# A two-stage transformer on one core: the opening takes scale and shift in quarters, turns x first, loads small vectors later, and multiplies constants in two waits of TensorE

## The reference

```python
cond = jax.nn.silu(c)
mod = cond @ ada_w[l] + ada_b[l]
sh1, sc1, g1, sh2, sc2, g2, sh3, sc3, g3 = jnp.split(mod, 9, axis=-1)
h = rms_norm(x, norm_ffn1[l]) * (1.0 + sc1) + sh1
x = x + 0.5 * (1.0 + g1) * ((jax.nn.silu(h @ ffn1_w1[l]) * (h @ ffn1_w3[l])) @ ffn1_w2[l])
...
```

## Time and profile before

| | |
|---|---|
| median of 3 runs | 2828.59 us (2826.72 to 2828.67) |
| the profiled execution, its time | 2824.73 us |
| its span | 2822.9 us |
| granted TensorE clock, mean | 0.99 |
| TensorE busy | 2754.0 us, 98% |
| VectorE busy | 2098.5 us, 74% |
| ScalarE busy | 1474.6 us, 52% |
| read from HBM | 516.94 MB |

### The profile page before, as it was taken

How to read it: one execution, slowest core, us unless ns; L and a number is a source line. 1 busy time by engine, 2 the same in 40 slices (tenths; PEclk the granted TensorE clock), 3 DMA queues, 4 the chain that set the end, 5 groups by cost and what they waited for, 6 DMA issues and landing times.

```text
span 2822.9 us, 53538 instructions
## 1 busy us (share of the span) xinstructions
PE 2754.0 (98%) x22660; PEld 2466.1 (87%) x22660; DVE 2098.5 (74%) x3313; ACT 1474.6 (52%) x2020; POOL 137.7 (5%) x257
## 2 busy tenths in 40 slices
PE   6999999999999998999999999999999999999998
PEld 6888899898888898998988988889888988898887
DVE  7887767779878877676886687755776677668774
ACT  3546654655455466446554465544654455446552
POOL 1000000200000000002000040000100000004000
PEclk7999999999999999999999999999999999999999
DMA  9775327548768753375585535555465557561652
GB/s 311 245 255 169 116 92 233 186 150 268 247 214 257 251 173 99 109 229 173 169 279 179 175 99 166 188 179 183 127 201 180 186 173 223 181 196 49 193 186 97
DMA packets 516702, 521.44 MB, mean 185 GB/s; under 512 B 16503, under 2 KB 513728, under 8 KB 516464
## 3 DMA queue, kind: packets, MB, share of 16 engines
q1 hardware_dynamic: 513856, 517.32, 57.0%
q0 software_dynamic: 816, 0.27, 0.1%
q10 hardware_dynamic: 1792, 0.44, 0.1%
HBM read 516.94 MB, written 1.05 MB: 183 GB/s over the span
## 4 chain that ended last, share of the span: by engine, by line
PE 89%; DVE 6%; ACT 3%; issue 1%; DMA 1%; ACTq 0%; POOL 0%; DVEq 0%
PE P L66 87%; PE P L69 2%; DVE arena L83 2%; ACT arena L72 1%; DVE wsp L75 1%; ACT wsp L72 1%; DVE arena L75 1%; DVE ACC L83 1%; ACT L72 0%; DVE HX L83 0%; DMA raw<-in_ada_w 0%; ACTq L104 0%; DMA arena<-in_norm_ffn 0%; DVE arena L95 0%; DVE arena L89 0%
## 5 line engine op out<-in xcount | busy, mean ns | idle before, releaser
L66 PE MATMUL P<-HX,wsp 128*128 128x512 f32 (+1 forms) x9920 | 1532.7, 316 | 12.0 <-DVE wsp L75 6.9
L66 PEld LDWEIGHTS P<-HX,wsp 128*128 128x128 f32 x9920 | 1382.0, 190 | 142.8 <-issue 14.3
L75 DVE TENSOR_TENSOR wsp<-raw,wsp 128x2048 fp32r<-128x2048 f32 (+4 forms) x454 | 947.3, 2090 | 291.9 <-ACT wsp L72 290.9
L72 ACT ACTIVATE wsp<-raw 128x2048 fp32r<-128x2048 f32 (+4 forms) x454 | 793.2, 1750 | 482.5 <-PE P L66 407.9
L66 PE MATMUL P<-FG,wsp 128*128 128x256 f32 (+1 forms) x2816 | 496.4, 337 | 0.0
L66 PEld LDWEIGHTS P<-FG,wsp 128*128 128x128 f32 x2816 | 428.7, 188 | 63.0 <-DVE wsp L75 1.2
L72 ACT ACTIVATE arena<-P 128x512 f32<-128x512 f32 (+3 forms) x375 | 207.5, 569 | 475.0 <-PE P L66 457.1
L75 DVE TENSOR_TENSOR arena<-arena,P 128x512 f32<-128x512 f32 (+2 forms) x226 | 146.9, 652 | 162.3 <-ACT arena L72 135.3
L83 DVE SCALAR_TENSOR_TENSOR ACC<-raw,sm,ACC 128x256 f32<-128x256 f32 x476 | 230.9, 485 | 16.8
L66 PE MATMUL P<-GX,wsp 128*128 128x256 f32 (+1 forms) x1592 | 229.4, 303 | 0.8 <-DVE GX L75 0.8
L66 PE MATMUL P<-arena 64*64 64x64 f32 (+9 forms) x4064 | 215.1, 263 | 13.5 <-DVE arena L75 4.7
(11 more groups left out here) (117 smaller groups left out, 1490.4 us busy)
## 6 DMA issues: line engine op xcount, KB each, us to landing
raw<-in_ffn_w SPq DMA_DIRECT2D x120, 1024.0 KB, 5.4
raw<-in_ada_w SPq DMA_DIRECT2D x72, 1024.0 KB, 5.1
raw<-in_w_in SPq DMA_DIRECT2D x52, 1024.0 KB, 5.2
raw<-in_ffn_w_gate SPq DMA_DIRECT2D x44, 1024.0 KB, 5.3
raw<-in_ffn_w_up SPq DMA_DIRECT2D x44, 1024.0 KB, 5.3
raw<-in_ffn_w_down SPq DMA_DIRECT2D x32, 1024.0 KB, 4.9
raw<-in_nsa_w_in SPq DMA_DIRECT2D x20, 1024.0 KB, 5.3
raw<-in_ffn_w SPq DMA_DIRECT2D x16, 768.0 KB, 4.2
```

Source lines behind the costliest of these rows:

```text
L66: return self if self.e is None else self.e.matmul(*a, skip_group_check=True, **k)
L72: return self if self.e is None else self.e.activation(*a, **k)
L75: return self if self.e is None else self.e.tensor_tensor(*a)
```

## The change

It is a reordering of the program's first part, and of the list of units there.

- The list begins with two ada units, then f1 and f3 of block 0, six more ada units, f1 and f3 of blocks 1 and 2, and so on. The first eight ada units alternate between a quarter of the scale (reduced by VectorE) and the same quarter of the shift (fresh, on TensorE).
- Norm 0 becomes `early`: blocks 0, 1 and 2 of the first feed-forward run on `XB` with `three`, block 0 quarter by quarter as scale and shift arrive (`first_pe`, `first_act`, `first_dve`). The normalised h is made behind block 1 and used from block 3 on.
- Tile 0 of the small vectors is now only c, the first bias and three gains, issued on SP behind x; TensorE turns x first and tile 0 between its sixth and seventh piece. All other small vectors and the positions are issued by GpSimd behind the eighth ada unit's add, and all five other tiles are turned ahead of block 5, where the cosine and sine are made as well.
- `busy_pe` multiplies the identity by 256 constant columns into a bank that nobody reads: five times behind the sums of squares, four times behind the spread.
- The later ada units of this feed-forward move one or two blocks back.

```diff
@@ part_of, fresh, plan_ffn @@
+            if j < 8:
+                return j // 2 if j % 2 else 4 + j // 2
...
-            return j < 8 and j % 2 == 0
+            return j < 8 and j % 2 == 1
...
-                if ada and (i % 4 and i < 11 if f else i % 4 != 3 and i < 10):
+                if f == i == 0:
+                    plan_ada(6)
+                elif ada and (i % 4 and i < 11 if f else i in (2, 4, 5, 6, 8, 9, 10)):
...
-                    if ada and s == 0:
+                    if ada and (s == 0 or f == 0 and s == 2 and q == 0):
...
-        plan_ada(8)
+        plan_ada(2)
@@ the start @@
         def start_act(e):
-            for t in range(3):
-                rows_dma(e, t)
-            e.dma_start(ALOG, ...
-            for t in (1, 2):
-                turned_act(e, t)
...
         def start_pool(e):
+            e.wait_ge(*AMOD.at(7))
             e.dma_start(posi, ...
-            for t in range(3, nrow):
+            for t in range(1, nrow):
                 rows_dma(e, t)
@@ the first block @@
+        def first_dve(e):
+            u = U["f1", 0][0]
+            for q in range(4):
+                ready_dve(e, U["ada"][2 * q], U["ada"][2 * q])
+                mod_dve(e, 2 * q)
+                low_dve(e, 0, q)
+                mod_dve(e, 2 * q + 1)
+                shift_pair_dve(e, q)
+                if q == 0:
+                    ready_dve(e, u, u + 1)
+            ready_dve(e, U["ada"][7], U["f1", 0][1])
+
+        def busy_pe(e, key, n):
+            b = take(e, ("busy", key))
+            for i in range(n):
+                e.matmul(P[b][:, 0:256], ident, C[:, 0:256], start=True, stop=True)
+            give(("busy", key))
+
+        def first_pe(e):
+            us = [U["f1", 0][0], U["f3", 0][0]]
+            sums_pe(e, 0)
+            busy_pe(e, "sums", 5)
+            for q in range(4):
+                ada_pe(e, 2 * q)
+                ada_pe(e, 2 * q + 1)
+                if q == 0:
+                    spread_pe(e, 0)
+                    busy_pe(e, "spread", 4)
+                    ps = [take2(e, (k, 0, 0)) for k in ("f1", "f3")]
+                for i in range(2):
+                    chunks_early(e, us[i], ps[i], 0, (2 * q, 2 * q + 1))
@@ ffn_pe, and likewise in ffn_act and ffn_dve @@
-                if i == 3 and f == 0:
-                    for t in range(3, nrow):
+                if i == 5 and f == 0:
+                    for t in range(1, nrow):
                         turn_rows(e, t)
...
+                        if n == 0 and i < 3:
+                            chunks_early(e, u, p, 0, range(8))
@@ sync_program @@
+            rows_dma(e, 0)
...
-                if u == 11:
+                if u == 15:
```

More of the change, by code:

```diff
@@ L658, in rows_dma @@
             st = ar(17152 + t * 128, 128)
-            e.wait_ge(*SET.at("rows"))
+            e.wait_ge(*SET.at("rows" if t else "row"))
             for base, c0, ap in prow[t][0]:
@@ L826, in mod_ready @@
         def mod_ready(l, part):
-            return AMOD.at(36 * l + part_of(4 * part + 3)) if part % 3 == 0 else AMOD.at(("part", l, part))
+            if l == 0 and part < 2:
+                return AMOD.at(("part", 0, 1, 3) if part else 7)
+            return AMOD.at(36 * l + 4 * part + 7) if part % 3 == 0 else AMOD.at(("part", l, part))
         SQ = ar(0, 8, 256)
@@ L889, in spread_pe @@
             ins.then_inc(*NSPR.up(n))
[L890 to L891 removed]
+            give(("nspr", n), NR_.at(n) if n < 14 else HT_.at((n, 3)))
         def root_act(e, n):
@@ L3102, in vector_program @@
             start_dve(e)
-            u = behind(-1)
-            for j in range(8):
-                mod_dve(e, j)
-                ready_dve(e, U["ada"][j], U["f1", 0][0] if j == 7 else U["ada"][7])
+            first_dve(e)
             for l in range(2):
-                norm_dve(e, 3 * l, u)
+                if l:
+                    norm_dve(e, 3 * l, u)
                 ffn_dve(e, 2 * l, 3 * l, (l, 0))
```

170 lines of the change are left out of this document (102 added, 68 removed).

## The result

The changed kernel takes **2833.88 us** (median of 20 runs, 2829.49 to 2837.56); the kernel before takes 2827.50 us beside it (20 runs, 2822.68 to 2830.41). The ratio is 1.0023, 95% interval 1.0017 to 1.0030: slower by 6.4 us, between 4.8 and 8.5. The profiled execution of the changed kernel took 2836.14 us (span 2834.3), 2.3 us over its own median, that of the kernel before 2824.73, 2.8 under the median of these 20. The two traces are therefore 11.4 us apart where the medians are 6.4 apart.

A forecast was written before the change was run, and what follows sets the result against it. TensorE is busy 98% of the span, so its dense start and later standstills count. The terms 0.7 + 1.9 + 6.7 + 2.0 = +11.3 us, added to 2828.6, give 2839.9 us, range 2830 to 2848.

The forecast's parts named there:

- Step 1: The opening up to block 1's start: 58.9 us against 58.19, so +0.7 us.
- the two kinds of work, which lay beside each other, are now one chain: Opening: ones-product, fresh product and VectorE's next reduction follow one another, 7.2 us a quarter at 2.4 GHz, 7.7 as mean.
- The constants: Constant products in the opening's waits: nothing taken; without any cover they would cost 6.2 us.
- Step 2: Blocks 1 and 2 on unscaled x, three products for two: +1.5 us; with one more ones-product, +1.9 us.
- Step 3: TensorE waits for banks at block 5: 7.7 us standing still in place of 1.0, so +6.7 us.
- L: Block 1's start in the new program, put at 58.9 us against 58.19 before.
- Step 4: Lower clock behind the wait at block 5: +2.0 us, between 0 and 2.4.
- The bounds: Lower and upper cases: block 1's start at 55.7 to 65.6 us, total time 2830 to 2848 us.
- the faster rival: Opening: fresh products' waits vanish into VectorE's work, block 1 starts at 46.5 us; total 2819 to 2823 us; chance 0.10.
- Slow throughout: Every burst of the opening at 1.2 GHz, constant products without effect: +19 us, 2848 us; chance 0.14.
- The small one: Opening quarters at 7.2 us, VectorE not late at block 5, no clock loss: 2832 to 2833.6 us; chance 0.14.

The follow-up runs named there:

- `pipelined`: The changed kernel with VectorE's reductions one quarter ahead and TensorE's ones-products ahead of the dense products; 2833.72 us, ratio 1.0031 to the kernel before.

## Why the prediction was right, and where its sizes were off

The prediction had 2839.9 us, a range of 2830 to 2848 and 0.76 on slower. Direction, place and mechanism held; the size was too large against the medians (+6.4 us, at most 8.5, for +11.3). Against the pair of traces (11.4 us apart) it looks exact, and that is partly luck: 1.2 us of these are the scatter behind norm 1, and two errors cancel in steps 3 and 4. The terms, as the traces have them:

| Step | predicted, us | measured, us |
|---|---|---|
| 1. start of block 1 | +0.7 | +0.2 |
| 2. products on XB, four units | +1.5 | +0.35 |
| 2. one more ones-product | +0.33 | +0.33 |
| 3. standing still at block 5 | +6.7 | +5.2 (3.61 + 2.54 - 0.99) |
| 4. clock behind it | +2.0 | +3.4 (7.41 + 7.37 - 2 x 5.7) |
| turning five tiles, not three | 0 | +0.2 |

That is 9.7 of the 10.2 us at norm 1.

**Step 1.** The date was right to 0.5 us (58.4 for 58.9), its working only in part. The chain began 1.1 us earlier than taken (reciprocal at 15.15 us for 16.2). Reductions came 6.9 and 7.5 us apart for the 7.7 taken (30.66, 37.54 and 45.07 in the trace), then the last ones-product was 1.6 us late, and the last low half came at 53.64 for 54.2. Block 1's start isn't a row of its own; from 192 products at 0.1207 us ahead of 81.57 it comes out at 58.4. The step that failed is "the two kinds of work, which lay beside each other, are now one chain": at the higher clock the fresh product ends with the low half of x, and the product put first made the quarters longer. Only a slow fresh product is part of the chain, by 1.6 us. What fills the rest of a quarter is TensorE's own burst at the lower clock, which pushed the ones-product from 49.1, when the fourth reduction had ended, to 50.73.

**The constants** at nothing: the times show no difference either way, and the 4.63 and 3.59 us they took lay in waits. What they give in quarter 0 in most executions is under 1 us at block 3, within its scatter.

**Step 2** took 0.127 us for a product from one short row. A long run of them took 19.92 us for 165, 0.1207 each, so a unit costs 0.1 us more than before, not 0.4.

**Step 3** named the pairs, the two waits (3.4 and 4.4 predicted, 3.61 and 2.54 measured) and their releasers. VectorE's lateness was right; the second wait was shorter because f1, which had to be done first, ran partly at the lower clock (7.41 us for 5.7), and because the copies came at L + 60.6 for the L + 61.2 taken. **Step 4** was charged once, where two waits cost a slow start each; a slow start that falls into a wait shortens it, so the two errors cancel in part: 8.7 us predicted for steps 3 and 4, 8.6 measured.

**The bounds**, added again: with every burst slow, L is 31.8 + 30.3 + 5.2 = 67.3, not 65.6, and the upper end of the range some 2 us higher; in the faster rival it is 44.5 + 3.05 = 47.5, not 46.5. Neither changes which rival fell.

**The rivals.** Slow throughout fell, with quarters of 7.5 and 8.7 us for 10.1. The burst of quarter 0 ran at 0.14 us a product, that of quarter 1 at 0.19, the clock coming back in it, that of quarter 2 at 0.23, slow to its end. The rule of the Trainium skill ("TensorE: Matmul & The Clock Gate", HAM oscillation) that I weighed has each tile start at the lower clock where its products are shorter than the wait for the next. The trace agrees for the bursts of quarters 1 and 2 (PEclk 0.50 at 37.77 and at 45.30 us) and not for every such burst: in `pipelined` the one at 55.35, behind the same 0.79 us of waiting, took 3.11 us at PEclk 1.00. Faster fell with quarter 3's shift at 53.6, not before 45. The small one lies nearest to the median, for a reason it did not have.

**What stays open.** Of 10.2 us at norm 1 in the traces, the medians keep 6.4 (7.7 where the changed kernel ran again). The kernel before was profiled in one execution 2.8 us under its median, and no second trace of it exists. The openings scatter by 1 to 2 us and the stretch behind norm 1 by 6 us, which is room enough for the difference, but no run settles it. Nor does one say why one program shows waits of 3.59 and 2.54 us with two slow starts in four executions and of 3.6 to 3.9 and 1.4 to 1.5 us with one longer slow start in two.

## What to carry to other kernels

A copy that frees a bank belongs ahead of any long work on its engine, and several small tiles that are turned together belong in one bank: each remedy alone took 4.4 us off the stretch here, both together 7.2. Before an opening is cut into finer pieces, add up every engine's own work per piece; here VectorE's cycle was 6.9 us and TensorE's 7 to 9, and no reordering of either moved block 3 ahead of its scatter, while getting the first input in earlier was worth 1 to 2 us with a much smaller edit. To judge a part of a long program, date two landmarks around it, in more than one execution: six executions of one stretch of 168 us fell into two groups, 0.06 and 0.3 us wide and 1.2 us or more apart, where the total scatters by 3 us to each side. And a date from one execution explains nothing of a median of eleven.

## What the runs showed of the hardware

- Standstills of TensorE and the slow products behind them, against 5.7 us for each unit: 3.59 to 3.90 us cost 1.6 to 2.8 (copies first, the changed kernel, `pipelined`), 3.03 cost 2.4 (rotation at block 3), 2.66 cost 2.7 (two banks), 2.54 cost 1.7. Those of 0.97, 1.42, 1.54 and 2.07 us cost 0.1 at most.
- With the five constants quarter 0's fresh product took 2.0 to 2.4 us in seven of nine executions and 3.6 in two, at start dates of 19.3 to 20.4 us. The same program differs by up to 2.1 us at block 3, and not by this alone: the latest of seven, 81.93, had a fast one.
- The granted clock's column does not always fit the durations. In the kernel with the quarters undone it reads 1.00 from 20 to 25 us, while the fresh product there (22.73) took 3.58 us, the duration it has at 0.50 elsewhere:

```profile
20.00:25.00 5.00, 2.68 (x52) 2.63 (x52) 3.58 (x10) 0.00 (x0) 0.00 (x0) 1.00 1.10 348
```

- GpSimd took some 0.5 us for each issue of a small transfer in the changed kernel (0.49 to 0.60 in its timeline, 0.74 for the positions), SP 0.30 us for those of 4 and 36 KB, against the 0.42 of x.
